# Wide products with one bank per 128 features in three mixers, with a reordered first stage and norms, and a mask moved to GpSimd

## What is computed

```python
def first_block(x, ...):                      # two layers
    h = x
    for layer in range(2):
        hn = rmsnorm(h, mix_norm[layer])
        if layer % 2 == 0:                    # "even": MoBA heads and NSA heads, relative bias
            h = h + moba_nsa_mixer(hn, ...)
        else:                                 # "fox": 16 heads with a forget gate
            h = h + fox_mixer(hn, ...)
        h = h + sqrelu_mlp(rmsnorm(h, mlp_norm[layer]), mlp_w1[layer], mlp_w2[layer])
    return rmsnorm(h, final_norm)

def second_block(x, c, ...):                  # one layer, modulated by c
    mod = silu(c) @ w_ada + b_ada             # nine rows: shifts, scales, gates
    h = x
    h = h + 0.5 * gt1 * swiglu(modulate(rmsnorm_2(h, g_ffn1), sh1, sc1), w1_gate, w1_up, w1_down)
    h = h + gt2 * hybrid_mixer(modulate(rmsnorm_2(h, g_mix), sh2, sc2), ...)   # "dil": pool and dilated heads
    h = h + 0.5 * gt3 * swiglu(modulate(rmsnorm_2(h, g_ffn2), sh3, sc3), w2_gate, w2_up, w2_down)
    return rmsnorm_2(h, g_final)
```

## Time and profile before

| | us |
|---|---|
| median of three runs | 1121.64 |
| the profiled execution | 1123.69 |
| its span in the trace | 1121.9 |
| TensorE busy | 1086.5 |
| VectorE busy | 783.7 |
| ScalarE busy | 648.2 |
| GpSimd busy | 98.6 |

### The profile page before, as it was taken

One profiled execution on the slowest core, in us unless ns is written; L12 is line 12 of the kernel. 1 busy time (PEld: TensorE's weight loads), 2 busy tenths in 40 slices (PEclk: granted clock), 3 DMA queues, 4 the chain that ended last, 5 costly groups with the idle time before them and its releaser, 6 DMA issues.

```text
span 1121.9 us, 15908 instructions
## 1 busy us (share of the span) xinstructions
PE 1086.5 (97%) x6118; PEld 922.1 (82%) x6118; DVE 783.7 (70%) x1275; ACT 648.2 (58%) x1048; POOL 98.6 (9%) x195
## 2 busy tenths in 40 slices
PE   6999999999999999999999999999989999999997
PEld 5888878888887997888888778888878978888885
DVE  6567767777777666776766768887875766665565
ACT  6656766555566776664645664444455767444443
POOL 1022210010000121100000001101000110000000
PEclk9999999999999999999999999999999999999999
DMA  7742248888855633677778547777644434555551
GB/s 301 289 155 83 102 141 308 292 292 297 295 201 183 246 130 114 235 268 248 266 259 313 193 143 289 264 295 288 220 153 150 152 117 154 190 190 187 189 190 60
DMA packets 39515, 236.71 MB, mean 211 GB/s; under 512 B 4453, under 2 KB 4613, under 8 KB 16528
## 3 DMA queue, kind: packets, MB, share of 16 engines
q1 hardware_dynamic: 26640, 188.76, 46.9%
q0 software_dynamic: 12512, 46.26, 11.6%
q10 hardware_dynamic: 288, 0.68, 0.2%
HBM read 234.58 MB, written 1.10 MB: 210 GB/s over the span
## 4 chain that ended last, share of the span: by engine, by line
PE 84%; DVE 7%; ACT 5%; issue 2%; DMA 2%; SPq 0%; DVEq 0%; ACTq 0%
PE bank L1451 21%; PE bank L1420 15%; PE bank L1422 14%; PE bank L1421 14%; PE bank L1452 11%; PE bank L1625 2%; DMA raw<-in_stream 2%; DVE w_lo L981 1%; ACT w_hi L631 1%; PE bank L1607 1%; DVE w_lo L970 1%; PE bank L1596 1%; PE bank L1519 1%; ACT w_hi L620 1%; PE bank L1595 1%
## 5 line engine op out<-in xcount | busy, mean ns | idle before, releaser
L1451 PE MATMUL bank<-a_two,w_hi 128*128 128x512 f32 x1088 | 386.3, 398 | 0.0
L981 DVE TENSOR_TENSOR w_lo<-raw,w_hi 128x2048 fp32r<-128x2048 f32 x123 | 278.5, 2289 | 109.1 <-ACT w_hi L631 109.1
L1452 PE MATMUL bank<-a_two,w_lo 128*128 128x256 f32 x1088 | 305.2, 281 | 0.0
L631 ACT ACTIVATE w_hi<-raw 128x2048 fp32r<-128x2048 f32 x123 | 232.1, 1909 | 49.7 <-DMA raw<-in_stream 49.7
L1451 PEld LDWEIGHTS bank<-a_two,w_hi 128*128 128x128 f32 x1088 | 204.4, 188 | 49.6
L1452 PEld LDWEIGHTS bank<-a_two,w_lo 128*128 128x128 f32 x1088 | 205.4, 189 | 1.7
L1420 PE MATMUL bank<-w_lo,hid_hi 128*128 128x512 f32 x432 | 169.6, 393 | 3.6 <-DVE w_lo L981 2.4
L1421 PE MATMUL bank<-w_hi,hid_lo 128*128 128x512 f32 x432 | 168.5, 390 | 0.0
L1422 PE MATMUL bank<-w_hi,hid_hi 128*128 128x512 f32 x432 | 168.5, 390 | 0.0
L797 ACT ACTIVATE cross<-bank 128x256 f32<-128x256 f32 x136 | 44.8, 382 | 203.7 <-PE bank L1452 203.7
L970 DVE TENSOR_TENSOR w_lo<-raw,w_hi 128x1024 fp32r<-128x1024 f32 x102 | 124.5, 1238 | 31.3 <-ACT w_hi L620 30.5
(11 more groups left out here) (212 smaller groups left out, 1489.2 us busy)
## 6 DMA issues: line engine op xcount, KB each, us to landing
raw<-in_stream SPq DMA_DIRECT2D x173, 1024.0 KB, 5.0
ada_raw<-in_ada POOLq DMA_DIRECT2D x72, 512.0 KB, 5.2
cmpw<-in_stream SPq DMA_DIRECT2D x4, 1024.0 KB, 8.4
rel_band<-rel_scratch POOLq DMA_DIRECT2D x2, 1024.0 KB, 10.9
cum_row<-cum_scratch POOLq DMA_DIRECT2D x4, 512.0 KB, 7.2
h<-in_x SPq DMA_DIRECT2D x2, 512.0 KB, 6.5
raw<-in_stream SPq DMA_DIRECT2D x2, 512.0 KB, 7.6
silu_row<-in_c_row POOLq DMA_DIRECT2D x2, 512.0 KB, 4.6
```

The lines of the kernel that those rows point to most:

```text
L631: nc.scalar.activation(w_hi[:, u % RING, :], raw[:, u % RING, :], ACT.Copy).then_inc(hi_ready, 2)
L981: nc.vector.tensor_tensor(w_lo[:, u % RING, :], raw[:, u % RING, :], w_hi[:, u % RING, :].bitcast(F32), ALU.subtract).then_inc(lo_ready, 2)
L1451: nc.tensor.matmul(ps[bank][:, 0:2 * T], wh[:, k, cols_], a_two[:, :, k, :], start=k == 0, stop=False)
L1452: ins = nc.tensor.matmul(ps[bank][:, T:2 * T], wl[:, k, cols_], a_hi[:, k, :], start=False, stop=k == KT - 1)
```

## The change

1. **Queries and keys.** The 19 units of `STACKS` use `wide_part`, the first 128 features into bank 4 and the second into bank 5. ScalarE copies half a bank (`cross_half`), VectorE makes the sum (`sum_half`), ScalarE copies the high part from it to where the heads read it (`stack`, four copies of 64x256 per half for keys, two for queries), and VectorE subtracts. A bank is taken again when its own sum is made (`feat_summed`). `kcvc` moves to bank 7.
2. **Wide units of the MLPs** finish one bank before the other, and the first is announced by `half_done`, so that its copy can begin half a unit earlier.
3. **Fox mask.** The product with the triangle goes. GpSimd adds the triangle to `cum_row` (and `cum_early` for the first 128 tokens), two additions of 128x(4x128) per DMA, between the DMAs.
4. **Norms.** ScalarE scales both halves of the rows, in pieces of 256, 256 and 512. The second half's squares stand between the pieces of `turned`. One dependent operation goes out of the root's chain, and VectorE's subtraction for a coming unit stands behind the second chain instead of ahead of it. Gf1's second root is taken later.
5. **First stage.** Thirty products of zeros run first. The first unit is used for both halves of the rows before the second, the roundings are placed between the pieces of `turned`, and the large constants are loaded by SyncE behind four units instead of by ScalarE at once.
6. **Smaller moves.** The SiLU of c goes from before unit F 2 to behind F 3 and the modulation columns begin a unit later; steps of the compressed heads move by a tick (nq1 part 3 to qm0 part 0, and others); the last stage's row parts change places, and the output is stored in quarters from two queues.

The diff, cut to its core:

```diff
@@ STACKS
-        STACKS = {("kskw", 0): (5, True, 4), ("nq0", 0): (4, False, 4), ("nq1", 0): (5, False, 6),
+        STACKS = {("kskw", 0): (True, 4), ("nq0", 0): (False, 4), ("nq1", 0): (False, 6),
...
+        STACK_BANKS = (4, 5)
@@ gpsimd
+            def mask(c):
+                pool.wait_ge(cum_landed[c], 16)
+                four = slice(4 * c, 4 * c + 4)
+                tri = pc_("tri", P).unsqueeze(1).to_broadcast([P, 4, P])
+                pool.tensor_tensor(cum_early[:, four, :], cum_row[:, four, 0:P], tri, ALU.add).then_inc(masked, 1)
+                pool.tensor_tensor(cum_row[:, four, P:T], cum_row[:, four, P:T], tri, ALU.add).then_inc(masked, 1)
...
-            for c in range(4):
+            for c in range(5):
+                if c < 4:
+                    if c > 0:
+                        pool.wait_ge(unit_used, FIRST["qk_fox"] + c - 1)
+                    pool.dma_start(cum_row[:, 4 * c:4 * c + 4, :], ...).then_inc(cum_landed[c], 16)
                 if c > 0:
-                    pool.wait_ge(unit_used, FIRST["qk_fox"] + c - 1)
-                pool.dma_start(cum_row[:, 4 * c:4 * c + 4, :], ...).then_inc(cum_landed[c], 16)
+                    mask(c - 1)
             scale(*FOX)
@@ scalar
             def norm_turn(name, gain, shift=None):
-                for t in range(TT):
-                    squares(name, t)
-                    if t == 0:
-                        round_half()
-                        scale(name)
-                    turned(name, t, gain, shift)
-                    if t == 0:
-                        round_half()
+                squares(name, 0)
+                round_half()
+                scale(name, 0)
+                turned(name, 0, gain, shift, (0, 1))
+                square_half(name, 1, 0)
+                turned(name, 0, gain, shift, (2, 3))
+                square_half(name, 1, 1)
+                round_half()
+                root(name, 1)
+                scale(name, 1)
+                turned(name, 1, gain, shift)
...
+            def cross_half(kind, key, nt):
+                n = STACK_NO[key]
+                keys = STACKS[key][0]
+                if nt == 0:
+                    act.wait_ge(half_done, HALF_BEFORE[kind] + n - STACKS_BEFORE[kind] + 1)
+                else:
+                    act.wait_ge(unit_used, FIRST[key[0]] + key[1] + 1)
+                nc.scalar.activation(cross[:, 0, nt, :], ps[STACK_BANKS[nt]][:, T:2 * T], ACT.Copy,
+                                     scale=1.0 if keys else -0.125).then_inc(feat_crossed, 1)
...
-            act.dma_start(par[:, COLS["pool_scale"]:N_COLS], cols[:, COLS["pool_scale"]:N_COLS]).then_inc(par_landed, 16)
             act.wait_ge(dve_step, 1)
+            gain0 = pc_("mix0", KT)
             squares("mix0", 0)
             round_half()
-            round_half()
             act.wait_ge(norms_landed, 16)
-            turned("mix0", 0, pc_("mix0", KT))
+            turned("mix0", 0, gain0, chunks=(0,))
             round_half()
             squares("mix0", 1)
@@ vector
+            def sum_half(key, nt):
+                keys = STACKS[key][0]
+                dve.wait_ge(feat_crossed, 2 * STACK_NO[key] + nt + 1)
+                nc.vector.scalar_tensor_tensor(out=cross[:, 1, nt, :], in0=ps[STACK_BANKS[nt]][:, 0:T], scalar=1.0 if keys else -0.125,
+                                               in1=cross[:, 0, nt, :], op0=ALU.mult, op1=ALU.add).then_inc(feat_summed, 1)
...
                 turned(name, 0, gain, shift, (2, 3))
-                rest_half()
...
                     inverse_root(name, 1)
-                scale(name, 1)
+                rest_half()
                 turned(name, 1, gain, shift)
@@ tensor
             def wide_unit(u, banks):
-                for half in range(2):
-                    for nt in range(2):
-                        wide_part(u, banks[nt], nt, (half,))
+                for nt in range(2):
+                    wide_part(u, banks[nt], nt)
...
-                if kind == "fox":
-                    ins = nc.tensor.matmul(bank[:, P:3 * P], ident_r[:, :], tri_r[:, :].unsqueeze(1).to_broadcast([P, 2, P]),
-                                           start=False, stop=True)
...
             def stacked_feature(tick):
                 n = STACK_NO[(tick.tag, tick.j)]
-                if tick.part == 0 and n >= 2:
-                    pe.wait_ge(feat_taken, 2 * (n - 1))
-                feature_part(tick.u, STACKS[(tick.tag, tick.j)][0], tick.part, tick.parts)
+                nt, part = divmod(tick.part, tick.parts // 2)
+                if part == 0 and n > 0:
+                    pe.wait_ge(feat_summed, 2 * n - 1 + nt)
+                wide_part(tick.u, STACK_BANKS[nt], nt, (0, 1) if tick.parts == 2 else (part,))
...
+            pe.wait_ge(zeros_set, 1)
+            for _n in range(WARM):
+                nc.tensor.matmul(ps[0][:, 0:P], probT[:, 0, 0:P], probT[:, 0, 0:P], start=True, stop=True)
+            pe.wait_ge(norms_landed, 16)
+            turn_rows("mix0", 0)
...
+            first_value = partial(value_part, "mix0", "v_even", parts=4, width=V1W)
+            first_value(j=0, part=0)
+            first_value(j=0, part=1)
+            turn_rows("mix0", 1)
+            pe.wait_ge(rel_rows_sb, 1)
+            first_value(j=0, part=2)
+            first_value(j=0, part=3)
+            for part in range(4):
+                first_value(j=1, part=part)
```

356 lines of the change are left out of this document (216 added, 140 removed).

## The result

The changed kernel takes 1125.55 us (median of 20 runs, 1123.12 to 1127.63), the kernel before 1121.71 in 20 runs on the same chips. The ratio is 1.0032, with a 95% interval of 1.0025 to 1.0039: slower by 0.3%, within the 0.5% that was called "same". The forecast was 1105.2, in a range from 1096 to 1114, with 0.89 for faster. The profiled execution has a span of 1124.8 us.

What follows compares the result with a forecast made beforehand. TensorE, busy 97% of the span, was taken to bound the kernel. The seven parts summed to -16.5: 1123.7 - 16.5 = 1107.2, less 2.05 to the median = 1105.2 us, range 1096 to 1114.

Steps and rivals of the forecast that it cites:

- Part 7: Mixers: new copies and sums per half unit on ScalarE and VectorE cost +3.0 us, bounds 0 and 11.
- rival B: Mixers: ScalarE becomes the bound, nearly half its extra work comes out on TensorE; 1113.2 us, chance 0.12.
- Part 2: Queries' and keys' units in the mixers: wide products save 0.10 us per unit over 19 units, -1.9 us.
- Part 3: Fox scores: dropping the mask product gives -2.7 us; one wait for GpSimd's masking and first scaling costs +2.8.
- Part 1: First stage and what follows: earlier third value unit, no `pair` wait, no low clock near 50; -8.0 us.
- Part 4: Norms: shorter waits for scaled rows (-4.5) and split rows (-1.8), together -6.3 us.
- Parts 5 and 6: MLP starts: fewer waits for low weights, -2.0 us; small ones: the `hid` wait and the kernel's end, -1.4.
- A: First stage: loads, helpers or a low clock keep the start from moving, gain 2 not 8.0; 1111.2 us, chance 0.12.
- C: Mixers: TensorE waits for its bank's sum at each of 38 halves, 0.6 us each; slower, 1124.9 us, chance 0.06.

Runs made afterwards that it cites:

- narrow_all: Changed kernel with the old 256-column form of the queries' and keys' units put back in all three mixers; 1113.50 us, ratio 0.9932 to the kernel before.
- best_te: Changed kernel with the old queries' and keys' form in all mixers, fourteen warm-up products and the fox mask back on TensorE; 1112.18 us, ratio 0.9915.
- best_inter: Changed kernel with the old queries' and keys' form, fourteen warm-up products, and GpSimd's masking interleaved with the first heads' scalings; 1110.42 us, ratio 0.9901.
- narrow_even: Changed kernel with the old 256-column form of the queries' and keys' units put back in the even mixer alone; 1118.36 us, ratio 0.9973.
- silu_early: Changed kernel with the SiLU of c and the load of its input back at the start of both MLPs; 1127.54 us, ratio 1.0045.
- best_narrow: Changed kernel with the old queries' and keys' form in all three mixers and fourteen warm-up products, mask still on GpSimd; 1113.54 us, ratio 0.9927.
- mask_te: Changed kernel with the fox mask given back to TensorE as a product per head, no additions on GpSimd; 1122.45 us, ratio 1.0003.
- warm14: Changed kernel with fourteen warm-up products instead of thirty; 1123.29 us, ratio 1.0013.

## Why the prediction was wrong

The forecast was -16.5 against the span; the median came out at +3.8. The miss of 20 us splits by the runs in two halves. Without the wide form (narrow_all) the change gives -7.6, where parts 1 and 3 to 6 had -17.6. The wide form adds 11.2, where parts 2 and 7 had +1.1.

1. **Part 7 is the term that failed most.** I priced the extra work at 3.0 (and 11 as bound, rival B). The amount of work was right: ScalarE is busy for 692.0 us against 665.7 in narrow_all, 26 more where I had 24. What failed is how much of it TensorE meets. I had read the load over a whole fox unit; the largest loss stood in the even mixer, in the ticks with the compressed attention, where VectorE has 2.5 us of its steps, and where the new steps come in the middle of a unit. I had no row of those ticks. A mean over a unit doesn't show them. 6.6 of the 11.2 is the even mixer's units: heads 0 to 23 are 6.3 shorter without the wide form, and the wait for `blk` ahead of head 0, 1.6, is gone (the two profiles differ by more than the medians do). The other 4.6 are in the fox and dilated mixers, and the masking enters there. An estimate of its share: with the mask on TensorE in both, the wide form costs (1.0003 - 0.9915) x 1121.7 = 9.9 less the 2.1 of the warm-up, 7.8, so some 3.4 of the 11.2 come only with GpSimd's additions.
2. **Part 2** was right in size: in the changed kernel half a wide unit takes 2.81 us (364.71 to 367.52), the unit 5.62, where 5.66 was forecast.
3. **Part 3.** The product is gone, and gives less than the 2.7 forecast: the fifteen steps between fox heads take 56.7 us in best_te and 54.6 in best_inter, 0.14 a head, so 2.3. The wait for GpSimd has the forecast size, 2.62, but it doesn't show in the changed kernel, since heads come late. In its place the additions hold VectorE's splits, a mechanism that I had not thought of. It cost 3.3 net of the products, so between 5.5 and 6, where I had written +2.8.
4. **Part 1** gave 4.1 instead of 8.0. The list of VectorE's work held: with fourteen warm-up products the third unit starts at 21.84 (21.2 forecast). What failed is that I took the warm-up as filling idle time and didn't cost it. Thirty products end at 10.05, where the turn can start at 7.92: 2.1 us in all. The clock near 50 did stay at 1.00 in this profile. `pair`'s wait did go, but one for `blk`, 1.6, stands in its place: VectorE's `blk` is behind a split, and the split behind ScalarE's copies of the half. With the old form in the even mixer that wait is under 0.15 (narrow_even) or 0.44 (narrow_all), so part 7's work took back what this step had given.
5. **Part 4** (-6.3) gave about 3.7 by the waits: the second half's scaled rows 5.8 to 2.7, where I had 1.3 left, the first half's 0.9 to 0.6, and the split rows, priced at -1.8, 3.3 to 3.0. At the norm before the first GLU, the kernel before and then the changed one:
```profile
638.58 1.03 PE L1519 MATMUL bank<-par,tok 128*128 128x128 f32 x8
641.06 0.47 PE L1420 MATMUL bank<-w_lo,a_two 128*128 128x512 f32 x1 [1.45 <-DVE a_two L1061]
```
```profile
642.77 1.03 PE L1648 MATMUL bank<-par,tok 128*128 128x128 f32 x8
645.25 0.47 PE L1549 MATMUL bank<-w_lo,a_two 128*128 128x512 f32 x1 [1.45 <-DVE a_two L1173]
```
In both the turn starts without a wait, right behind TensorE's own last products, and the split rows come 2.48 us after it. The root chain, which the change shortens, had been done: it is not on this path. I took a wait for what its engine does and didn't look at whether the turn itself had waited.
6. **Parts 5 and 6.** The waits near 187 and 488 are gone, and silu_early brings both back. The end behind the last product gives 0.3 of the 0.5. The wait for `hid_lo`, 1.1, which was in no part, is gone too. But low weights are late elsewhere: 1.4 before the norm of the first GLU, which was 0.8. In runs with the same code there it lies between none (best_narrow, best_te) and 1.7 (mask_te), so it moves with what stands ahead. And 0.9 is in two new waits in that GLU: the second root of gf1, which the change took later, stands on VectorE from 696.36 to 697.19, ahead of the subtraction that the first of them waits for. No run took that apart.
7. **The rivals.** A (start doesn't move) and B (helpers become the bound in the mixers) both came true in part, together with the hold between GpSimd and VectorE, which was in none. C's mechanism, a wait for the bank's sum at each half, occurred once. I had noted that A and B together end near 1119 and left that out of the range.

What stays open: how the 6.6 in the even mixer splits between the two helpers, since the dose on each cost something and moving the steps changed nothing; whether it is the length or the operands of GpSimd's operations that VectorE meets; and why some of TensorE's waits are followed by a low clock and others aren't. Behind the changed kernel's own 2.58 and 2.16 the granted clock stayed at 1.00, behind the same two waits in warm14 (2.58 and 2.20) it fell both times, and in narrow_all it is at 0.50 from 82.6 to 86.0 with no wait over 0.15 us since 47.

## What to carry to other kernels

Before work is moved to an engine beside the critical one, read the single ticks in which that engine is fullest, not its share over a unit; and ask of each new operation where its operands lie, since one with two operands in SBUF can be held by another engine's. Price filler work as work: it ends when it ends. Test a change of several parts by taking back one at a time: here one part of it carried a loss of 11 us and the rest a gain of 8, and the rest with two corrections beats both kernels.

## What the runs showed of the hardware

- An operation of GpSimd on SBUF and one of VectorE with two operands in SBUF hold each other up: a pair of splits of 0.85 took 3.29, 2.44, 2.51 and, with twice the additions, 4.95 us, and an addition of 1.09 took 2.07. Beside operations of 0.61 to 0.64 us the pairs took at most 1.22. A sum with one operand in a bank took its usual 0.42 beside an addition (372.28).
- GpSimd takes 1.09 us for an addition of two operands of 128x512, and 0.61 to 0.64 for the same size with one, plain or as a select by position.
- A wait of TensorE can cost twice where TensorE is the path: the wait of 2.6 in best_narrow and the 3.5 us at a granted clock of 0.53 behind it cost 4.1. Stretches of 3 to 7 us at 0.50 to 0.53 stand behind or at waits of 0.9 to 4.1 us in most of the profiles, behind the same wait in one run and not in another, and in narrow_all without a wait.
- Where the helpers are the path, the low clock cost nothing: 6.8 us of it in the even mixer left heads 0 to 23 at 79.3 us.
- At the start TensorE ran at half pace, 0.43 us for 512 columns, until 18.7 us in the kernel before (first product at 8.68) and 16.7 without warm-up (7.79); with warm-up products from 1.05 on the pace doubled at 5.3 and 4.2. The profile has no clock record before those times and shows 1.00.
